# One level of Strassen's scheme in the feed-forwards of a hybrid decoder layer: gate and up products of two thirds of the tokens

## What is computed

```python
def rmsnorm(x, g):
    xf = x.astype(jnp.float32)
    y = xf * lax.rsqrt(jnp.mean(xf * xf, axis=-1, keepdims=True) + EPS)
    return (y * g.astype(jnp.float32)).astype(x.dtype)

def swiglu(x, w_gate, w_up, w_down):
    return (jax.nn.silu(x @ w_gate) * (x @ w_up)) @ w_down

def layer(x, sc_buf, gdn_buf, gdn_s, segments, w):
    ...
    x = x + 0.5 * swiglu(rmsnorm(x, n_f1), f1_g, f1_u, f1_d)
    ...
    x = x + merged @ w_o
    x = x + 0.5 * swiglu(rmsnorm(x, n_f2), f2_g, f2_u, f2_d)
```

## Time and profile before

| what | value |
|---|---|
| time, median of 3 runs | 3458.63 us (3454.99 to 3458.74) |
| span of the profiled execution | 3453.9 us |
| PE busy | 3322.5 us, 96% |
| DVE, ACT, POOL busy | 38%, 29%, 26% |
| mean granted clock of PE | 0.975 |
| feed-forward 1: first ACT operation to last POOL operation | 24.3 to 835.0 us |
| feed-forward 2, the same | 2616.2 to 3428.6 us |

### The profile page before, as it was taken

How to read it: one execution, slowest core, us unless ns; L and a number is a source line. 1 busy time by engine, 2 the same in 40 slices (tenths; PEclk the granted TensorE clock), 3 DMA queues, 4 the chain that set the end, 5 groups by cost and what they waited for, 6 DMA issues and landing times. The chain is left out here.

```text
span 3453.9 us, 51790 instructions
## 1 busy us (share of the span) xinstructions
PE 3322.5 (96%) x20286; PEld 3236.0 (94%) x20286; DVE 1326.3 (38%) x2186; ACT 1013.5 (29%) x1408; POOL 891.1 (26%) x506
## 2 busy tenths in 40 slices
PE   8999999998999799999999999879999999999998
PEld 8999999998999699899999998769999999999998
DVE  4333333334777433333333333333223333333333
ACT  5111111114222354444444454321024111111113
POOL 2121121214122333323333333212233121111112
PEclk9999999999999899999999999779999999999998
DMA  4111111112222212112112121354312111111111
GB/s 135 40 49 43 43 43 43 43 43 79 73 86 88 81 51 69 58 51 68 58 51 75 51 69 36 99 195 151 120 38 74 43 43 49 43 43 43 36 30 52
DMA packets 274431, 222.74 MB, mean 64 GB/s; under 512 B 12042, under 2 KB 251786, under 8 KB 274288
## 3 DMA queue, kind: packets, MB, share of 16 engines
q1 hardware_dynamic: 273988, 220.56, 21.0%
q10 hardware_dynamic: 324, 0.41, 0.0%
HBM read 170.66 MB, written 50.28 MB: 64 GB/s over the span
## 5 line engine op out<-in xcount | busy, mean ns | idle before, releaser
L209 PE MATMUL ffn_bank<-ffn_h_hi,ffn_w_hi 128*128 128x368 f32 x2112 | 698.2, 331 | 6.8 <-DVE ffn_h_lo L618 6.8
L210 PE MATMUL ffn_bank<-ffn_h_lo,ffn_w_hi 128*128 128x368 f32 x2112 | 699.2, 331 | 0.0
L211 PE MATMUL ffn_bank<-ffn_h_hi,ffn_w_lo 128*128 128x368 f32 x2112 | 697.9, 330 | 0.0
L209 PE MATMUL mix_bank<-mix_h_hi,mix_w_hi 128*128 128x368 f32 x1752 | 639.5, 365 | 6.6 <-DVE mix_pre L1750 3.2
L408 POOL TENSOR_TENSOR ffn_w_lo<-g_w_raw,ffn_w_hi 128x1024 fp32r<-128x1024 f32 x130 | 310.9, 2400 | 1191.4 <-ACT ffn_w_hi L404 1191.3
L210 PE MATMUL mix_bank<-mix_h_lo,mix_w_hi 128*128 128x368 f32 x1752 | 580.3, 331 | 0.0
L211 PE MATMUL mix_bank<-mix_h_hi,mix_w_lo 128*128 128x368 f32 x1752 | 579.0, 330 | 0.0
L209 PEld LDWEIGHTS ffn_bank<-ffn_h_hi,ffn_w_hi 128*128 128x128 f32 x2112 | 398.3, 189 | 8.1 <-issue 8.0
L211 PEld LDWEIGHTS ffn_bank<-ffn_h_hi,ffn_w_lo 128*128 128x128 f32 x2112 | 398.0, 188 | 0.0
L210 PEld LDWEIGHTS ffn_bank<-ffn_h_lo,ffn_w_hi 128*128 128x128 f32 x2112 | 397.8, 188 | 0.1
L817 POOL TENSOR_TENSOR mix_w_lo<-g_w_raw,mix_w_hi 128x1024 fp32r<-128x1024 f32 x73 | 186.0, 2549 | 782.0 <-ACT mix_w_hi L812 782.0
(11 more groups left out here) (242 smaller groups left out, 4559.5 us busy)
## 6 DMA issues: line engine op xcount, KB each, us to landing
g_w_raw<-in_w_in SPq DMA_DIRECT2D x73, 512.0 KB, 6.0
g_w_raw<-in_ffn_w_gate SPq DMA_DIRECT2D x44, 512.0 KB, 3.8
g_w_raw<-in_ffn_w_up SPq DMA_DIRECT2D x44, 512.0 KB, 3.8
g_w_raw<-in_ffn_w_down SPq DMA_DIRECT2D x44, 512.0 KB, 3.5
scratch_qkv<-mix_out SPq DMA_DIRECT2D x24, 552.0 KB, 2.8
turn_kq<-scratch_qkv SPq DMA_DIRECT2D x32, 256.0 KB, 3.9
scratch_x<-g_x SPq DMA_DIRECT2D x8, 552.0 KB, 7.2
scratch_z<-turn_z_out SPq DMA_DIRECT2D x8, 552.0 KB, 2.8
```

The costliest lines, as they stand in the source:

```text
L209: pe.matmul(out, w_hi, x_hi, start=first, stop=False)
L210: pe.matmul(out, w_hi, x_lo, start=False, stop=False)
L211: return pe.matmul(out, w_lo, x_hi, start=False, stop=last)
```

## The change

For the first two thirds of the tokens (1 and 2) the gate product of a group, and likewise the up product, is seen as a 2 x 2 product: two halves of the tokens, two halves of the 1024 features, two units of 128. Seven products of quarter size (P1 to P7, Winograd's form of Strassen's scheme) take the place of eight. The last third is done plainly, as four quarter products (Z1a, Z1b into one bank, Z2a, Z2b into another). Each of these 11 steps is 4 blocks x 3 passes = 12 matmuls; two pairs (gate, up) make 22 steps, 264 matmuls, for 288. Down keeps its 144.

What is new around it:

- **Tokens.** The combinations S1 to S4 of token blocks need x times gain times factor, so the factor comes first. DVE writes the 8 scaled blocks (`raw`, one operation with two SBUF inputs), then DVE (S1, S2, S4) and POOL (S3) combine them. Nine blocks of 4 x 368 = 1472 columns are split: ACT makes the high halves, DVE the low halves of A11, Z1, A12, Z2, S2 and S3, POOL those of A22, S1 and S4. All this is done once, in the first group.
- **Weights.** Each gate or up pair uses eight operands of 512 columns: quarters B11, B21, B12, B22 and combinations T1 to T4, which DVE makes by subtraction. With four quarters for down a group has 20 operands. Each is split by ACT (high) and POOL (low) into a ring of five. The raw slots are still three.
- **Results.** ACT copies P1, DVE adds the others bank by bank in the order U2, U3, C22, C21, C12 (one input in PSUM, one in SBUF), ACT takes the silu, DVE multiplies (`up_sum`, `up_bank`), and high and low halves follow per part: 11, Z1, 22, 21, Z2, 12. PE waits for five of these before its first part of down and for the sixth before its third. Down runs over the thirds as 2, 1, 0.
- **Queues.** ACT splits the down quarters 14 to 17 before the high half of part 22, quarter 18 after it, and quarter 19 after the high half of part 12. In the last group PE waits for the last quarter before any part of down.
- **First group.** The steps that need no combination come first, for both pairs: P1 gate, P1 up, Z1a of both, P2 of both, Z1b of both, then the rest of gate, then the rest of up. The raw units loaded ahead are gate 0, gate 1 and up 0; up 1 is loaded after T4 of gate is split, down 0 after B22 of gate, down 1 after T4 of up.

The core of the diff (the lines of before that go can be read above):

```diff
+PAIR_OPS = ("B11", "B21", "T2", "B12", "T3", "T1", "T4", "B22")
+PAIR_STEPS = ("P1", "Z1a", "P2", "Z1b", "P6", "Z2a", "P7", "P5", "P4", "Z2b", "P3")
+LAST_READER = {"B11": "Z1a", "B21": "Z1b", "T2": "P6", "B12": "Z2a", "T3": "P7", "T1": "P5", "T4": "P4", "B22": "P3"}
+PRODUCTS = {"P1": ("a", "A11", "B11"), "P2": ("a", "A12", "B21"), "P6": ("b", "S2", "T2"), "P7": ("b", "S3", "T3"),
+            "P4": ("b", "A22", "T4"), "P5": ("c", "S1", "T1"), "P3": ("c", "S4", "B22"),
...
+        if first:
+            lead = [("g", "B11"), ("u", "B11"), ("g", "B21"), ("u", "B21")]
+            self.ops = lead + [(p, n) for p in "gu" for n in PAIR_OPS[2:]] + DOWN_OPS
+            lead = [(p, n) for n in ("P1", "Z1a", "P2", "Z1b") for p in "gu"]
+            self.steps = lead + [(p, n) for p in "gu" for n in PAIR_STEPS[4:]]
...
+    def split_lo(self, pool, i, g, pair, name):
+        n = plan_of(i, g).op(pair, name)
+        pool.wait_ge(self.hi_done, i * N_OPS + (N_OPS * g + n + 1))
+        pool.tensor_tensor(self.lo[:, n % self.RING, :, :], self.source(pair, name), self.hi[:, n % self.RING, :, :].bitcast(F32),
                            ALU.subtract).then_inc(self.lo_done, 1)
-    def wait(self, pe, i, g, u):
-        pe.wait_ge(self.lo_done, i * self.UNITS + (self.UNITS * g + u + 1))
+    def combine(self, dve, i, g, pair, name):
+        if name == "T1":
+            self.wait_lo(dve, i, g, pair, "B11")
+            self.wait_raw(dve, i, g, (pair, "f2"))
+            a, b = "B12", "B11"
+        elif name == "T2":
+            dve.wait_ge(self.t_done, self.combined(i, g, pair, "T1"))
+            a, b = "B22", "T1"
+        elif name == "T4":
+            self.wait_lo(dve, i, g, pair, "B21")
+            dve.wait_ge(self.t_done, self.combined(i, g, pair, "T2"))
+            a, b = "B21", "T2"
+        else:
+            self.wait_lo(dve, i, g, pair, "B12")
+            a, b = "B22", "B12"
+        dve.tensor_tensor(self.source(pair, name), self.source(pair, a), self.source(pair, b), ALU.subtract).then_inc(self.t_done, 1)
...
+        HI_ORDER = ("A11", "A11", "A11", "A11", "Z1", "A12", "Z2", "A22", "S2", "S3", "S1", "S4")
+        LO_ORDER = ("A11", "A11", "A11", "A11", "Z1", "A12", "Z2", "S2", "S3")
+        LO_POOL_ORDER = ("A22", "S1", "S4")
+        MID_ORDER = ("11", "Z1", "22", "21", "Z2", "12")
...
+            def rest(i, g):
+                early = plan_of(i, g).op
+                load(i, g, ("u", "f2"), early("g", "T4") + 1)
+                load(i, g, ("d", "a0"), early("g", "B22") + 1)
+                load(i, g, ("d", "a1"), early("u", "T4") + 1)
+            def following(i, g):
+                for unit, pair, name in ((("g", "f1"), "u", "B22"), (("g", "f2"), "d", "01"), (("u", "f1"), "d", "11")):
+                    sp.wait_ge(w.lo_done, i * N_OPS + (N_OPS * g + STEADY.op(pair, name) + 1))
+                    load(i, g + 1, unit, None)
...
+            def block_lo(name):
+                pool.wait_ge(blk_hi, last(HI_ORDER, name))
+                src = raw_slot("S1", 0) if name == "A22" else raw_slot(name, 1)
+                pool.tensor_tensor(slot(name, 1), src, slot(name, 0).bitcast(F32), ALU.subtract).then_inc(blk_lo_pool, 1)
+            for pair, name in FIRST.ops:
+                w.split_lo(pool, 0, 0, pair, name)
+                if (pair, name) == ("u", "B21"):
+                    pool.wait_ge(raw_h, KC // 2)
+                    pool.tensor_tensor(raw_slot("S3", 1), raw_slot("S2", 0), raw_slot("S3", 0),
+                                       ALU.subtract).then_inc(combo_pool, 1)
+                    block_lo("A22")
+                elif (pair, name) == ("g", "T3"):
+                    block_lo("S1")
+                elif (pair, name) == ("g", "B22"):
+                    pool.wait_ge(combo, 3)
+                    block_lo("S4")
             with pool.Fori(0, GROUPS - 1) as i:
-                for u in (4, 5):
-                    w.split_lo(pool, i, 0, u)
-                for u in range(4):
-                    w.split_lo(pool, i, 1, u)
-            for u in (4, 5):
-                w.split_lo(pool, 0, GROUPS - 1, u)
+                for pair, name in STEADY.ops:
+                    w.split_lo(pool, i, 1, pair, name)
...
+            def mid_wait(i, g, at):
+                if at == 0:
+                    pe.wait_ge(mid_ready, i * 6 + (6 * g + last(MID_ORDER, "Z2")))
+                elif at == 2:
+                    pe.wait_ge(mid_ready, i * 6 + (6 * g + last(MID_ORDER, "12")))
...
+            w.wait_lo(pe, 0, GROUPS - 1, "d", "11")
+            for at, b in enumerate(THIRD_ORDER):
+                mid_wait(0, GROUPS - 1, at)
...
+            def first_product(i, g, pair):
+                k = 3 * (pair == "u")
+                stepped(act, i, g, pair, "P1")
+                dst = mid(sums_buf if pair == "u" else hid, "21")
+                act.copy(dst, bank[k][:, 0:TH]).then_inc(free[k], 1)
...
+            def first_group():
+                for kc in range(KC // 2):
+                    split_hi(0, 0, kc)
+                    act.wait_ge(raw_h, kc + 1)
+                    block_hi("A11", kc)
+                block_hi("Z1")
+                first_product(0, 0, "g")
+                first_product(0, 0, "u")
+                act.wait_ge(raw_h, KC)
+                block_hi("A12")
+                block_hi("Z2")
+                block_hi("A22")
+                gate_from_bank(0, 0, "11")
+                act.wait_ge(combo, 2)
+                act.wait_ge(combo_pool, 1)
+                act.wait_ge(blk_lo, 4)
+                block_hi("S2")
+                split_hi(0, 0, 4)
+                block_hi("S3")
+                split_hi(0, 0, 5)
+                gate_from_bank(0, 0, "Z1")
+                split_hi(0, 0, 6)
+                act.wait_ge(blk_lo_pool, 1)
+                block_hi("S1")
+                for n in (7, 8, 9):
+                    split_hi(0, 0, n)
+                act.wait_ge(combo, 3)
+                block_hi("S4")
...
+            def up_rest(i, g):
+                mid_high(i, g, "11")
+                mid_high(i, g, "Z1")
+                for n in range(14, 18):
+                    split_hi(i, g, n)
+                mid_high(i, g, "22")
+                split_hi(i, g, 18)
+                mid_high(i, g, "21")
+                mid_high(i, g, "Z2")
+                mid_high(i, g, "12")
+                split_hi(i, g, 19)
...
+            for b in range(NB):
+                fac.log(act, bank[b] if partial else None, b)
             fac.root(act)
+            first_group()
...
+            def raw(k):
+                at = 0 if k < KC // 2 else 3
+                kc = k % (KC // 2)
+                dve.scalar_tensor_tensor(h_raw[:, at:at + 3, kc * TH:(kc + 1) * TH],
+                                         x[:, k, :].rearrange("p (b t) -> p b t", b=NB), gains[:, g_at, k:k + 1],
+                                         rstd[:, :].rearrange("p (b t) -> p b t", b=NB), ALU.mult, ALU.mult).then_inc(raw_h, 1)
...
+            def read(i, g, pair, name, buf, a, b, reads):
+                k = bank_of(i, g, pair, PRODUCTS[name][0])[0]
+                stepped(dve, i, g, pair, name)
+                dve.tensor_tensor(mid(buf, a), bank[k][:, 0:TH], mid(buf, b), ALU.add).then_inc(free[k], 1)
...
+            def up_sum(i, g, name):
+                k, reads, at = {"22": (5, 1, 0), "21": (4, 3, 1), "12": (5, 2, 2)}[name]
+                freed(dve, i, g, k, reads)
+                dve.wait_ge(silu_done, i * 3 + (3 * g + at + 1))
+                out = mid(hid, name)
+                dve.tensor_tensor(out, mid(sums_buf, name), out, ALU.mult).then_inc(up_done, 1)
+            def mid_low(i, g, name):
+                dve.wait_ge(mid_hi_done, i * 6 + (6 * g + last(MID_ORDER, name)))
+                dve.tensor_tensor(mid(mid_lo, name), mid(hid, name), mid(mid_hi, name).bitcast(F32), ALU.subtract) \
+                    .then_inc(mid_ready, 1)
...
+            def up_late(i, g):
+                sums(i, g, "u", "U2")
+                sums(i, g, "u", "U3")
+                sums(i, g, "u", "C22")
+                up_sum(i, g, "22")
+                mid_low(i, g, "22")
+                sums(i, g, "u", "C21")
+                up_sum(i, g, "21")
+                mid_low(i, g, "21")
+                up_bank(i, g, "Z2")
+                mid_low(i, g, "Z2")
+                sums(i, g, "u", "C12")
+                up_sum(i, g, "12")
+                mid_low(i, g, "12")
...
+            raw(0)
+            raw(1)
+            block_lo("A11", 0)
+            raw(2)
+            block_lo("A11", 1)
+            raw(3)
+            block_lo("A11", 2)
+            block_lo("A11", 3)
+            raw(4)
+            block_lo("Z1")
+            for k in (5, 6, 7):
+                raw(k)
+            block_lo("A12")
+            dve.wait_ge(raw_h, KC)
+            combine_h("S1", raw_slot("S3", 0), raw_slot("S1", 0), ALU.add)
+            block_lo("Z2")
+            dve.wait_ge(combo, 1)
```

(94 more changed lines are left out.)

407 lines of the change are left out of this document (225 added, 182 removed).

## The result

The changed kernel takes **3470.14 us** (median of 5 runs, 3466.39 to 3472.37) against 3455.05 for the kernel before in the same set (5 runs, 3453.3 to 3458.74): a ratio of 1.004 (95% interval 1.0027 to 1.0052). It is slower by 15 us; 3472 was forecast, and slower had the best chance.

The account below looks back on a forecast made before the run. The prediction took a middle group to be bound by PE's number of matmuls. Middle -46.4, first +59.7 and last 0 gave +13.3 on the span of 3453.9, so 3467.2; with 4.7 for the median 3472 us, range 3428 to 3494.

Parts of the forecast that it names:

- Removed matmuls: In 22 groups, 24 matmuls go per group, 528 at 0.1679 us: 88.6 us saved, all on the path.
- Middle groups: Eighteen groups: each saves 4.03 us less a stall of 1.45 before down; together -46.4 us (-36 to -58).
- its worse bound: Middle groups: if the 18th weight quarter collides too, the stall is 1.8 to 2.0 us and the gain 2.0.
- Last groups: Two last groups: down starts 4.6 us late, taking the saved 4.03, and the drain keeps its length: 0 (-1 to +1).
- First groups: Two first groups: factor before products, 54.3 us of DVE and POOL work through one port; +29 and +30.5, together +59.7.
- 8 us of idle time before P6 of gate: First group: sign that PE would idle 8 us there, released by POOL, if the forecast held.
- The rule for the port: Two-input DVE work and POOL work share one resource, and DVE without a pause keeps it; 2.00 us where 0.54 is usual.
- The low bound of the starts: First groups if the work shares nothing: end at R+82 to 84, so +10 and +13, 23 us in all.
- Rival 1: First groups: POOL gets in at gaps between DVE operations; starts cost +23 in place of +59.7, time 3435; chance 0.28.
- Rivals 2 and 3: Rival 2: middle stall 2.0 us, starts +66, 3489, chance 0.17. Rival 3: no middle stall, starts +23, 3409, chance 0.08.
- allowance of 0.15: Middle groups, before down: 0.15 us for PE's restarting, part of the 1.45 us stall.

Follow-up runs that it names:

- single edits: Two separate edits of the changed kernel: block factor written to PSUM, 3463.2 us; POOL's first-group S3 and three low halves replaced by fills, 3457.32 us.
- The plain first group: Changed kernel with each feed-forward's first group done by the 288 products of before, S1 to S4 made while PE is in that group: 3423.68 us.

## Why the prediction was right, step by step

The difference of +13.3 us came out as +15.1 between the medians and +16.7 between the profiled executions, and the parts came out nearly as added up. That 3472 is within 2 us of 3470.14 is luck in part: the profiled span was 3.4 above the forecast of 3467.2, and the 4.7 that the prediction added for the median was -0.5 this time (3470.14 against 3470.6).

- **Removed matmuls, 88.6 us: right.** The period of 69.81 is 408 matmuls and a gap of 1.3: 68.5/408 is 167.9 ns again. The formula that the Trainium skill (TensorE: Matmul & The Clock Gate, Back-to-back issue gap) gives for a product alone makes, as an estimate, 155.8 ns and 63.6 us for 408; no period here comes near that.
- **Middle groups, -46.4: right** (-46.6). The stall of 1.1 and its cause, quarter 18 against part 21's product, stood in the prediction: 1.08 there, 1.04 in the trace, and 1.15 us for a product that was given 1.1. The second feed-forward also shows the collision of quarter 17 that was its worse bound: in its second group the product of part 22 takes 1.34 us at 2773.58 and the period is 71.82, the longest of the nine, whose mean is 70.09.
- **Last groups, 0: +0.3 and +1.4.** PE's 4.3 us of idle time came as worked out (4.6). The +1.4 lies outside the bound of 1. Left out was the clock: behind that idle time PE was granted 0.71 from 811.1 to 817 us, a mean of its levels of 1.2 and 2.4 GHz, and the 24 adds took 24.7 instead of 22.7 us. Most of it hid behind POOL's sums, which did not keep their length, though: 28.1 and 28.3 us for 26.8.
- **First groups, +59.7: right in size** (+62.7; 103.99 us from the first scaled block, forecast 102.9; R is the start of that block). P6 of gate started at R+38.8 (40.6 forecast), P5 at R+48.9 (49.3), P6 of up at R+59.7 (60.4). After that one wait was missed: Z2a of up stood 2.65 us for the bank that DVE had still to read, then ran at the lower clock (3.6 for 2.0 us), and P3 of up ended at R+78.2 (74.5); the middle chain, less disturbed than forecast, gave 2.8 of that back. The sign that the prediction gave for this, 8 us of idle time before P6 of gate released by POOL, did not come: PE stood 2.35 us there. It was late by itself, after 7.8 us of waits for low halves of token blocks (L869) after its first product and 15 us at the lower clock, of which the prediction had only "part of it at half clock".
- **The rule for the port was wrong in one step**: "up's first quarter gets the port only when DVE waits for ACT, at R+15.0". POOL had it at R+3.7 and ended at R+4.8 (35.45); the two engines took turns, operation by operation, and both were stretched (DVE 2.38 for 1.36, POOL 1.93 and 2.28 for 1.28) where the prediction had stretched POOL's alone. The sum of both engines' work, 54 us through one port, is the same in any order; that this is why the total stood is argued, not shown.
- **Two figures of the prediction do not come out of its own terms.** ACT's 0.52 us for 512 columns is 0.62 on the line of the two values beside it, and 0.63 on average in the trace (L735, 396 times). The low bound of the starts, R+82 to 84, is 8.4 to 10.4 and 9.6 to 11.6 us, about 20 together and not 23, so rivals 1 and 3 were priced some 3 us too high. The first is worth at most 0.1 us in a middle group; the second enters no sum of the forecast.
- **Rival 1** (starts under 20 us each) needed POOL to pass beside DVE; it passed in turns instead, and the starts cost 30.2 and 32.5. Rivals 2 and 3 fell with the periods 69.8 and 70.1: between 69 and 70.3.

What stays open is the rest of the start's loss, 31 us less the 3.5 and 7 that single edits took away. It is not all the port. The 2.65 us before Z2a of up were a bank. The 2.48 us before P6 of up end a chain that begins with a load: DVE stood 2.35 us for the unit up 1, which landed at 84.7, and POOL then split T2 in its usual 1.27; of this chain only 0.4 us are a meeting at the port (T1, 1.07 for 0.69). And in the first feed-forward PE's work took 10.4 us more than at 167.9 ns each, at the lower clock, where it was 1.6 before; how much of that other waits would have taken up, no run here shows. The plain first group shows that the loss goes, but for 8.3 us in the first feed-forward, when the combinations leave the path, not by which of their costs.

## What to carry to other kernels

Fewer multiplications pay only where the sums that replace them find room: here the scheme earned 2.7 and 2.4 us in a middle group of the two feed-forwards and lost it all in two first groups, so let the first pass run in the old form while the operands of the new one are made behind it. Count DVE operations with two SBUF inputs and POOL operations that read SBUF as one engine's work wherever they can meet, and put one input in PSUM, or the smaller work a few us later, where they do. When a trace names the engine that ended a wait, look whether that engine had long been done. An operand that is wanted 12 us into a phase should not be prepared ahead of the chain that opens the phase.

## What the runs showed of the hardware

A fill by POOL does not hold DVE, a subtraction does: 0.53 and 1.69 us for DVE's operations beside fills, 3.62 and 4.84 beside subtractions of the same buffers. The Trainium skill (SBUF — State Buffer, Who interferes with whom) says just this, that a two-input DVE operation contends with a GpSimd operation that reads SBUF and not with one that only writes it, and the rows agree. The Trainium skill (SBUF — State Buffer, Summary: rules for kernel authors) also says that the second of the two to issue waits until the first has finished. The turns at 31.22 to 35.85 us agree; in the second pair of the earlier trace rows POOL waited for longer than one DVE operation, and no run here tells why.

PE's clock after a short pause was not the same each time. After 1.0 us of idle time before down it stayed at 1.00, and in the first group also after 2.35 us (to 69.45). In the second group of the second feed-forward, after 1.77 us, 0.64 was granted over the next 3.3 us, a mean of the levels of 1.2 and 2.4 GHz, and the adds took 24.1 instead of 22.7 us:

```profile
2780.70:2784.00 3.30, 3.30 (x14) 3.30 (x15) 1.89 (x5) 1.55 (x3) 1.23 (x1) 0.64 0.01 3
```

So this stall cost 1.4 us more than its length, which the prediction's allowance of 0.15 did not cover.
